# Scores of two attention kinds in the second token tile, computed in 64-row tiles of TensorE, both kinds at once

## The chip, the cores and the metric

The kernel runs on one core of a Trainium2 chip. The metric is device time in microseconds (us) of one launch, the median of three runs. A core has TensorE (PE in the profile, its weight loads PEld), VectorE (DVE), ScalarE (ACT), GpSimd (POOL) and SyncE (SP), each with an instruction queue of its own, tied to the others by semaphores alone.

## The reference

The launch computes two transformer blocks on 256 tokens in float32. Only the attention of the second block, run in each of its two layers, matters here. Its `nsa_mixer` has eight query heads over two key groups and three branches, compressed, selected and sliding:

```python
s = jnp.einsum('bqgrd,bgqmd->bgrqm', qi, kg).astype(jnp.float32) * scale   # selected
s = s - slopes[None, :, :, None, None] * dist_s
p_s = masked_softmax(s, mask_s)
o_s = jnp.einsum('bgrqm,bgqmd->bqgrd', p_s.astype(vg.dtype), vg)
s = jnp.einsum('bqgrd,bkgd->bgrqk', qi, kw).astype(jnp.float32) * scale    # sliding
...
o_w = jnp.einsum('bgrqk,bkgd->bqgrd', p_w.astype(vw.dtype), vw)
return gi[..., 0:1] * o_c + gi[..., 1:2] * o_s + gi[..., 2:3] * o_w
```

With 256 tokens both the selected and the sliding branch see every earlier key, so both are plain causal attention with a slope per head and 64 elements to a head (`NSA_DH = 64`). `mla_mixer` beside it is a third kind, with 96 elements to a head.

## The kernel before, in words

Every engine's program is written out by hand in one order. The 256 tokens are two tiles of 128 rows. The attention of a layer is a list of 26 units, `UNITS_2` (line 237), and each engine walks the list in a loop of its own, `attend`:

- K, the compressed branch, one unit for each tile;
- then for tile 0 the units S0 W0 S1 W1 S2 W2 S3 W3 M0 M1 M2 M3, then the same twelve for tile 1. S is the selected kind, W the sliding kind, M the latent kind; each unit has two heads. The position in the list, j, is 10 to 13 for M0 to M3 of tile 0, 14 to 21 for S0 to W3 of tile 1, and 22 to 25 for its M0 to M3. u is j plus an even offset.

A unit of tile 0 has 128 keys, one of tile 1 has 256. Its steps are: scores on TensorE into PSUM (line 1190, one matmul for each head; TensorE makes two passes of each float32 matmul, so the trace has two records for one matmul), logits on VectorE (2357, one instruction for each head adds the bias and takes the maximum; 2360 negates the maximum and announces `logits_ready`), exps on ScalarE (1692), turn on TensorE (1206, 128x128 transposes), copy out of PSUM on ScalarE (1702), value on TensorE (1232), output on VectorE (2403 reciprocal, 2413 gate, 2419 for S and W or 2421 for M).

The loops are staggered. TensorE does, for each j: scores(j), turn(j-2), value(j-3). VectorE does: logits(j), output(j-3). ScalarE does: copy(j-2), exps(j). The scores have two places in PSUM, 1024 columns each, used in turn (`(u % 2) * 1024`), so scores(j) waits for `logits_ready` of unit j-2: the place that it overwrites has been read.

Queries and keys of S and W lie on half of the partitions. `QTN` holds two heads in one tile, even head on partitions 0 to 63, odd head on 64 to 127; `KTN` holds for each head of a pair the keys on its own half and zeros on the other half. Before the change a matmul takes all 128 rows, zeros included. The two heads of a unit write to two halves of one PSUM bank (pitch 256 columns). M's heads take 96 of the 128 rows.

Elsewhere in the program (line 1337, the index scores of the first block) there are matmuls on 64 rows already: two heads on the two halves of the partitions, into two PSUM banks, 256 columns each, eight such pairs in the launch. They stand among full-height matmuls (1275) and transposes (1116).

Of the kernel before, what the change touches and what calls it, by code (L numbers as in the profile page):

```python
# [25 lines left out]
P = 128  # L26
# [6 lines left out]
HD = 64  # L33
# [51 lines left out]
G_LAYER = 26  # L85
# [131 lines left out]
def at(value, per, l):  # L217

    return value if l is None else value + per * l
# [5 lines left out]
def unit(kind, n, tile):  # L225

    keys = T if kind == "X" else 2 * NC if kind == "K" else P * (tile + 1)
    subs = 3 if kind == "A" else 4 if kind == "K" else 2

    return dict(kind=kind, n=n, tile=tile, keys=keys, subs=subs, pitch=512 if kind == "C" else keys, nk=1 if kind == "K" else keys // P,  # L230
                wide=kind == "A", mid=kind in "BKX")


# [6 lines left out]
U1, U2 = len(UNITS_1), len(UNITS_2) + len(UNITS_X)  # L240
# [7 lines left out]
def mids_before(u):  # L248
    return sum(x["mid"] for x in ALL_UNITS[:u])


def two_blocks_kernel(nc, a, out):
    ctx = ExitStack()
    with ctx:
# [3 lines left out]
        def sem(name):  # L258
            return ctx.enter_context(nc.semaphore(name))
# [14 lines left out]
        PS, PT, PO = ALL[:, 0:2048], ALL[:, 2048:3072], ALL[:, 3072:4096]  # L274
# [18 lines left out]
        def lbuf(x, u):  # L293

            if x["kind"] in "ABC":
                return w((W_L, W_L + 768, W_GB)[u % 3], 768)
            return w(W_L + 512 * (u % 3), 512)
# [24 lines left out]
        def ka(h):  # L322
            return QTA[:, 6 + h // 2, :] if h % 2 == 0 else P1[:, h // 6, T * (h // 2 % 3):T * (h // 2 % 3) + T]

        def qb(c):
            return P1[:, 0, 768 + c * T:768 + (c + 1) * T] if c < 3 else P1[:, 1, 768:1024]

        def kb(m):
            if m < 4:
                return P1[:, m % 2, C_BQ + T * (m // 2):C_BQ + T * (m // 2) + T]  # L330
            if m % 2 == 0:
                return P1[:, 1, 1024 + T * (m // 2 - 2):1024 + T * (m // 2 - 2) + T]
            return P1[:, m // 2 - 2, C_BQ + 512:C_BQ + 512 + T]

        def qc(n):
            return P1[:, n, C_CQ:C_CQ + T]
# [7 lines left out]
        def kc(s):  # L344
            return P1[:, s, C_BQ + 768:C_BQ + 1024]
# [47 lines left out]
        group_free = sem("group_free")  # L393
# [27 lines left out]
        scores_ready = sem("scores_ready")  # L421
        logits_ready = sem("logits_ready")
# [379 lines left out]
        def _(pe):  # L802
            mm = nc.tensor.matmul
# [295 lines left out]
            def branch_product(n, j, i, h, k, acts):  # L1099

                arrived(n)
                for c in range(k):
                    o = c * D + h * 512
                    last = mm(branch_bank(j, i, h), acts[:, c, i * P:(i + 1) * P], ring[:, n % RING, o:o + 512],  # L1104
                              start=(c == 0), stop=(c == k - 1))
                return last
# [36 lines left out]
            def query(x, s, i):  # L1143
                k, n = x["kind"], x["n"]
                q = slice(i * P, (i + 1) * P)
                if k == "A":
                    h = 4 * s + n
                    return [(QTA[:, h // 2, q], ka(h))]
                if k == "B":
                    h = 4 * s + n  # L1150
                    return [(qb(h // 2)[:, q], kb(h))]
                if k == "C":
                    return [(qc(n)[:, q], kc(s))]
                if k == "K":
                    return [(QTN[:, s, q], KBD[:, 30 * (s // 2):30 * (s // 2) + 30])]
                if k in "SW":
                    h = 2 * n + s
                    return [(QTN[:, h // 2, q], KTN[:, (4 if k == "S" else 8) + 2 * (h // 4) + h % 2, :])]
                if k == "M":
                    return [(QTM[:, 2 * n + s, q], KTM[:, 2 * n + s, :])]  # L1160
                return [(XQT[:, 4 * n + 2 * s + c, q], XK[n][:, 2 * s + c, :]) for c in range(2)]
# [17 lines left out]

            def attend(units, u0, l=None, between={}, behind_turn={}):  # L1180

                def scores(j):
                    x, u = units[j], u0 + j
                    if j >= 2:
                        pe.wait_ge(logits_ready, at(u - 1, U2, l))
                    for s in range(x["subs"]):
                        o = (u % 2) * 1024 + s * x["pitch"]
                        pairs = query(x, s, x["tile"])
                        for c, (q, k) in enumerate(pairs):
                            last = mm(PS[:, o:o + x["keys"]], q, k[:, 0:x["keys"]], start=(c == 0), stop=(c == len(pairs) - 1))  # L1190
                    last.then_inc(scores_ready, 1)

                def turn(j):
                    x, u = units[j], u0 + j
                    if x["mid"]:
                        pe.wait_ge(mixed_ready, at(mids_before(u) + 1, MIDS_2, l))
                    else:
                        pe.wait_ge(probs_ready, at(u + 1, U2, l))
                    single = x["wide"] or (j and units[j - 1]["wide"])
                    if j >= (1 if single else 2):  # L1200
                        pe.wait_ge(probs_out, at(u if single else u - 1, U2, l))
                    o = 0 if x["wide"] else (u % 2) * 512
                    for s in range({"B": 1, "K": 2}.get(x["kind"], x["subs"])):
                        for kb in range(x["nk"]):
                            c = s * P if x["kind"] == "K" else s * x["keys"] + kb * P
                            last = nc.tensor.transpose(PT[:, o:o + P], lbuf(x, u)[:, c:c + P], ident)  # L1206
                            o += P
                    last.then_inc(probs_turned, 1)

                def value(j):  # L1210
                    x, u = units[j], u0 + j
                    pe.wait_ge(probs_out, at(u + 1, U2, l))
                    if j >= 2:
                        pe.wait_ge(unit_done, at(u - 1, U2, l))
                    o = (u % 2) * 512
                    k = x["kind"]
                    if k == "X":
                        for c in range(4):
                            for kb in range(2):
                                n = 2 * (c // 2) + kb  # L1220
                                last = mm(PO[:, o + c * P:o + (c + 1) * P], XV[x["n"]][kb][:, c * P:(c + 1) * P],  # L1221
                                          PTS[:, u % 2, n * P:(n + 1) * P], start=(kb == 0), stop=(kb == 1))
                        last.then_inc(values_ready, 1)
                        return
                    dv = P if k == "B" else T if k == "K" else HD
                    blocks = [(s, kb) for s in range({"B": 1, "K": 2}.get(k, x["subs"])) for kb in range(x["nk"])]
                    for n, (s, kb) in enumerate(blocks):
                        pt = PTS[:, u % 2, n * P:(n + 1) * P]
                        first = n == 0 if k == "A" else kb == 0
                        final = n == len(blocks) - 1 if k == "A" else kb == x["nk"] - 1  # L1230
                        c = o if k == "A" else o + s * dv
                        last = mm(PO[:, c:c + dv], pt, values(x, s, kb), start=first, stop=final)  # L1232
                    last.then_inc(values_ready, 1)

                n = len(units)
                for j in range(n + 3):
                    if j in between:
                        between[j]()
                    if j < n:
                        scores(j)  # L1240
                    if 0 <= j - 2 < n:
                        turn(j - 2)
                    if j in behind_turn:
                        behind_turn[j]()
                    if 0 <= j - 3:
                        value(j - 3)
# [156 lines left out]
            for i in range(TT):  # L1403
                last = branch_product(P_BRA + 1, "c", i, 0, 2, XT[:, 6:8, :])
            last.then_inc(branch_done, 1)
            pe.wait_ge(branch_used, 1)
            for i in range(TT):
                last = branch_product(P_BRA + 1, "c", i, 1, 2, XT[:, 6:8, :])
            last.then_inc(panel_done, 1)
            pe.wait_ge(branch_used, 2)  # L1410
            for h in range(2):
                last = branch_product(P_BRA + 2, "b", 0, h, 4, XT[:, 2:6, :])
            last.then_inc(branch_done, 1)
            for h in range(2):
                last = branch_product(P_BRA + 2, "b", 1, h, 4, XT[:, 2:6, :])
# [18 lines left out]
            for l in range(LAYERS):  # L1434
# [91 lines left out]
                for g in range(2):  # L1526
                    last = mm(PO[:, 512 + g * HD:512 + (g + 1) * HD], HPAD[:, g, :], w2v, start=True, stop=True)
# [1365 lines left out]
```

## Time and profile before

| | us |
|---|---|
| median of three runs | 1697.09 |
| lowest, highest | 1696.93, 1698.31 |
| the profiled execution, its own time | 1696.81 |
| its span, first to last instruction | 1694.9 |
| TensorE busy (share of the span) | 1665.5 (98%) |
| VectorE busy | 1223.2 (72%) |
| ScalarE busy | 352.5 (21%) |
| mean granted TensorE clock | 0.998 |

The attention of the second block's first layer takes from about 831 us to 892 us of the span, that of the second layer from about 1313 to 1373 us. The profile has a record for each instruction, by engine and line. In the timeline a row's second number runs from the first start to the last end of the group, and matmul records overlap, since a matmul is started before the one ahead of it has drained: the spacing of starts tells what a matmul costs in a row of them. The chain of work that ended last counts each piece from the end of the piece before it, and so gives such costs directly.

### The profile page before, as it was taken

What the parts mean: (1) busy time and instruction counts of PE and PEld (TensorE: products, weight loads), DVE (VectorE), ACT (ScalarE), POOL (GpSimd) and SP (SyncE); (2) the same over time, 40 slices, a digit from 0 to 9 for tenths busy, and PEclk for the clock granted to TensorE, in tenths of its full rate; (3) what the DMA queues carried; (4) which work ended last, traced back from release to release, by engine and by line L of the source; (5) the groups of instructions that cost most, each with busy time, mean ns of one, the idle gap of its engine ahead of it and who ended that gap; (6) DMA issues with size and microseconds to landing.
All of it is one profiled execution on the core that took longest, in us unless ns stands there. A gap on an engine that the chain in (4) does not pass through costs nothing.

```text
span 1694.9 us, 22817 instructions
## 1 busy us (share of the span) xinstructions
PE 1665.5 (98%) x8726; PEld 1281.4 (76%) x8726; DVE 1223.2 (72%) x2230; ACT 352.5 (21%) x893; POOL 212.7 (13%) x139
## 2 busy tenths in 40 slices
PE   7999999999999999999999999999999999999998
PEld 6887488877847886477784969994687767699953
DVE  6777467976787777573376778996844685789995
ACT  2111000034511111112270212220012531222210
POOL 1222211121021212211001000002120000000021
PEclk9999999999999999999999999999999999999999
DMA  9685454524176555346513536444447206265440
GB/s 320 194 230 177 146 199 162 175 80 149 51 232 213 160 164 184 124 145 178 207 51 131 155 125 194 156 170 153 158 121 252 100 1 224 71 226 177 150 173 25
DMA packets 163755, 267.07 MB, mean 158 GB/s; under 512 B 4279, under 2 KB 106477, under 8 KB 163519
## 3 DMA queue, kind: packets, MB, share of 16 engines
q1 hardware_dynamic: 157902, 248.66, 43.8%
q0 software_dynamic: 5008, 15.91, 3.3%
q8 instruction: 70, 1.15, 0.3%
q10 hardware_dynamic: 736, 1.05, 0.3%
q14 instruction: 39, 0.31, 0.1%
HBM read 262.52 MB, written 2.03 MB: 156 GB/s over the span
## 4 chain that ended last, share of the span: by engine, by line
PE 90%; DVE 5%; DVEq 2%; issue 1%; ACT 1%; DMA 1%; SPq 0%; ACTq 0%
PE psum L1017 19%; PE psum L886 16%; PE psum L1065 13%; PE psum L952 12%; PE psum L844 7%; PE psum L1275 4%; PE psum L1481 3%; PE psum L1538 3%; PE psum L1190 3%; PE psum L1116 3%; PE psum L1232 2%; PE psum L825 2%; PE psum L1104 2%; PE psum L1206 1%; PE psum L1221 1%
## 5 line engine op out<-in xcount | busy, mean ns | idle before, releaser
L695 POOL TENSOR_TENSOR work<-ring,work 128x1024 f32<-128x1024 f32 (+2 forms) x59 | 147.4, 2499 | 791.5 <-DVE work L2199 791.5
L2191 DVE TENSOR_TENSOR work<-ring 128x1024 f32<-128x1024 f32 (+2 forms) x102 | 122.0, 1196 | 83.3 <-PE psum L1065 74.3
L1065 PE MATMUL psum<-ring,work 128*128 128x512 f32 x352 | 160.8, 592 | 0.0
L2195 DVE TENSOR_TENSOR ring<-ring 128x1024 f32<-128x1024 f32 (+2 forms) x104 | 131.7, 1267 | 7.7
L2199 DVE TENSOR_TENSOR work<-ring 128x1024 f32<-128x1024 f32 (+2 forms) x102 | 122.6, 1202 | 7.6
L1065 PEld LDWEIGHTS psum<-ring,work 128*128 128x128 f32 x352 | 66.4, 190 | 81.1 <-issue 79.9
L1065 PE MATMUL psum<-work 128*128 128x512 f32 x264 | 122.5, 592 | 0.0
L1017 PE MATMUL psum<-x_t,work 128*128 128x128 f32 x832 | 101.4, 275 | 0.0
L1017 PE MATMUL psum<-work,ring 128*128 128x128 f32 x832 | 101.4, 275 | 0.0
L1017 PE MATMUL psum<-x_t,ring 128*128 128x128 f32 x832 | 97.4, 275 | 1.6 <-ACT x_t L1610 1.6
L1017 PEld LDWEIGHTS psum<-x_t,work 128*128 128x128 f32 x832 | 97.1, 192 | 0.0
L1017 PEld LDWEIGHTS psum<-work,ring 128*128 128x128 f32 x832 | 97.1, 192 | 0.0
L1017 PEld LDWEIGHTS psum<-x_t,ring 128*128 128x128 f32 x832 | 95.0, 192 | 2.4 <-issue 2.4
L1065 PEld LDWEIGHTS psum<-work 128*128 128x128 f32 x264 | 49.7, 190 | 62.0 <-issue 60.3
L2823 DVE SCALAR_TENSOR_TENSOR work<-work 128x254 f32<-128x254 f32 (+1 forms) x176 | 83.5, 526 | 3.3
L886 PE MATMUL psum<-ring,work 128*128 128x256 f32 x352 | 83.2, 379 | 0.0
L886 PE MATMUL psum<-ring,x_t 128*128 128x256 f32 x352 | 81.7, 386 | 1.5 <-DMA ring<-in_ffn_w_gate_dram 1.3
L886 PE MATMUL psum<-work,x_t 128*128 128x256 f32 x352 | 82.9, 379 | 0.0
L1190 PE MATMUL psum<-work 128*128 128x256 f32 (+2 forms) x384 | 79.5, 338 | 0.3 <-DVE stat L2360 0.3
L886 PEld LDWEIGHTS psum<-ring,x_t 128*128 128x128 f32 x352 | 67.9, 194 | 12.2 <-DMA ring<-in_ffn_w_gate_dram 2.4
L1692 ACT ACTIVATE work<-work,stat 128x256 f32<-128x256 f32 (+1 forms) x136 | 61.6, 453 | 66.5 <-DVE stat L2360 65.6
L886 PEld LDWEIGHTS psum<-ring,work 128*128 128x128 f32 x352 | 66.9, 190 | 9.1
(304 smaller groups left out, 2865.6 us busy)
## 6 DMA issues: line engine op xcount, KB each, us to landing
ring<-in_ffn_w_up_dram SPq DMA_DIRECT2D x66, 1024.0 KB, 7.9
ring<-in_w_in_dram SPq DMA_DIRECT2D x21, 2048.0 KB, 7.9
ring<-in_ffn_w_down_dram SPq DMA_DIRECT2D x20, 2048.0 KB, 7.8
ring<-in_ffn_w_gate_dram SPq DMA_DIRECT2D x22, 1024.0 KB, 5.7
ring<-in_xa_wkv_dram SPq DMA_DIRECT2D x8, 2048.0 KB, 9.5
ring<-in_w_out_dram SPq DMA_DIRECT2D x6, 2048.0 KB, 10.9
ring<-in_xa_wq_dram SPq DMA_DIRECT2D x4, 2048.0 KB, 7.9
ring<-in_xa_wo_dram SPq DMA_DIRECT2D x4, 2048.0 KB, 11.3
```

Of the source, the lines that this page charges most:

```text
L695: nc.gpsimd.tensor_tensor(t4, quarters(n, chunks, pitch)[2], t2, ALU.subtract).then_inc(fourth_ready, 1)
L844: last = mm(share_bank(p), acts[p][:, q, :], rhs[:, i, :], start=(q == 0), stop=(q == KD // 2 - 1))
L886: last = mm(corners(j)[p], acts[p][:, i, :], rhs[:, i, :], start=(i == 0), stop=(i == KD // 2 - 1))
L952: last = mm(row_corners(j)[p][:, 0:pitch // 2], acts[p][:, i, :], rhs[:, i, :], start=(i == 0), stop=(i == KD // 2 - 1))
L1017: last = mm(corners(j)[p][:, c * P:(c + 1) * P], weights[:, i, c * P:(c + 1) * P], acts[p][:, i, :], start=(i == 0), stop=(i == KD // 2 - 1))
L1065: last = mm(sums[p], acts[p][:, q, :], rhs[:, i, :], start=(q == 0), stop=(q == KF // 2 - 1))
L1190: last = mm(PS[:, o:o + x["keys"]], q, k[:, 0:x["keys"]], start=(c == 0), stop=(c == len(pairs) - 1))
L1275: last = mm(row_corners(q + 1)[p], acts_of_gates[p][:, i, :], rhs[:, i, :], start=(i == 0), stop=(i == KD // 2 - 1))
L2191: v.tensor_tensor(t3, b22, b12, ALU.subtract)
L2195: v.tensor_tensor(b12, b12, b11, ALU.subtract)
L2199: v.tensor_tensor(t2, b22, b12, ALU.subtract).then_inc(forms_ready, 1)
L2823: last = v.scalar_tensor_tensor(dst, UP[:, q, 0:T - t], CWT[:, 2 - t, k:k + 1], dst, ALU.mult, ALU.add)
```

## The change

`unit` gives S and W units of tile 1 a pitch of 512 columns, so that the two heads of a unit write to two PSUM banks (0 and 1 for S, 2 and 3 for W). On TensorE, at the place of an S unit of tile 1, a new function issues the scores of that S unit and of the W unit behind it: four matmuls, each on 64 rows (the head's own half of the partitions, without the zeros). The W unit's own place issues no scores. The four matmuls wait for `logits_ready` of unit j-1 and for `group_free` (an earlier copy out of banks 1 and 3, made at the ninth unit ahead of them). Each unit still announces `scores_ready` behind its second matmul. Nothing changes on the other engines but the columns that the logits read.

```diff
-    return dict(..., pitch=512 if kind == "C" else keys, ...)
+    return dict(..., pitch=512 if kind == "C" or kind in "SW" and tile else keys, ...)
...
+                def scores_by_rows(j):
+                    u = u0 + j
+                    pe.wait_ge(group_free, at(H_WV + 2, G_LAYER, l))
+                    pe.wait_ge(logits_ready, at(u, U2, l))
+                    for t in (j, j + 1):
+                        x = units[t]
+                        for s in range(2):
+                            r = slice(HD * s, HD * s + HD)
+                            o = ((u0 + t) % 2) * 1024 + s * x["pitch"]
+                            (q, k), = query(x, s, 1)
+                            last = mm(PS[:, o:o + x["keys"]], q[r], k[r, 0:x["keys"]], start=True, stop=True)
+                        last.then_inc(scores_ready, 1)
+
                 def scores(j):
                     x, u = units[j], u0 + j
+                    if x["kind"] in "SW" and x["tile"]:
+                        if x["kind"] == "S":
+                            scores_by_rows(j)
+                        return
                     if j >= 2:
                         pe.wait_ge(logits_ready, at(u - 1, U2, l))
```

(`at(u, U2, l)` is the count of `logits_ready` when unit j-1 has announced; `at(u - 1, ...)` is that of unit j-2.)

TensorE's queue in the first layer, from the scores of S1 to those of S2 in tile 1, before:

```order
918 L1190 MATMUL psum<-work 128x256 [waits logits_ready]
919 L1190 MATMUL psum<-work 128x256
920 L1206 MATMUL psum<-ident_fours,work 128x128 [waits probs_out,probs_ready]
921 L1206 MATMUL psum<-ident_fours,work 128x128 x3
922 L1232 MATMUL psum<-work 128x64 [waits unit_done,probs_out]
923 L1232 MATMUL psum<-work 128x64 x3
924 L1190 MATMUL psum<-work 128x256 [waits logits_ready]
925 L1190 MATMUL psum<-work 128x256
926 L1206 MATMUL psum<-ident_fours,work 128x128 [waits probs_out,probs_ready]
927 L1206 MATMUL psum<-ident_fours,work 128x128 x3
928 L1232 MATMUL psum<-work 128x64 [waits unit_done,probs_out]
929 L1232 MATMUL psum<-work 128x64 x3
```

Every unit has its scores, then turn(j-2), then value(j-3). The same stretch after the change (lines are shifted: 1192 the new scores, 1223 turn, 1249 value):

```order
914 L1192 MATMUL psum<-work 128x256 [waits logits_ready,group_free]
915 L1192 MATMUL psum<-work 128x256 x3
916 L1223 MATMUL psum<-ident_fours,work 128x128 [waits probs_out,probs_ready]
917 L1223 MATMUL psum<-ident_fours,work 128x128 x3
918 L1249 MATMUL psum<-work 128x64 [waits unit_done,probs_out]
919 L1249 MATMUL psum<-work 128x64 x3
920 L1223 MATMUL psum<-ident_fours,work 128x128 [waits probs_out,probs_ready]
921 L1223 MATMUL psum<-ident_fours,work 128x128 x3
922 L1249 MATMUL psum<-work 128x64 [waits unit_done,probs_out]
923 L1249 MATMUL psum<-work 128x64 x3
```

The four score matmuls of a pair of units now stand together at its head, and the second unit's two have moved ahead of a turn and a value. (The shapes are those of the outputs; the rows that a matmul takes are not in this view.)

## Rows read from the trace of the kernel before

**Rows 1.** The page: span, busy time of TensorE and VectorE, the chain by engine.
```profile
span 1694.9 us, 22817 instructions
...
PE 1665.5 (98%) x8726; PEld 1281.4 (76%) x8726; DVE 1223.2 (72%) x2230; ACT 352.5 (21%) x893; POOL 212.7 (13%) x139
...
PE 90%; DVE 5%; DVEq 2%; issue 1%; ACT 1%; DMA 1%; SPq 0%; ACTq 0%
```

**Rows 2.** The chain in tile 1, first layer: start, us, what, records.
```profile
864.87 0.22 PE psum L1206 x2
865.08 0.39 PE psum L1232 x4
...
875.46 0.92 PE psum L1190 x4
876.38 0.44 PE psum L1206 x4
876.82 0.84 PE psum L1232 x8
877.66 0.92 PE psum L1190 x4
```

**Rows 3.** TensorE's timeline: start, us, engine line op, tiles, shape, records, [idle before].
```profile
863.78 1.08 PE L1190 MATMUL psum<-work 128*128 128x256 f32 x4
...
875.30 1.08 PE L1190 MATMUL psum<-work 128*128 128x256 f32 x4
876.22 0.60 PE L1206 MATMUL psum<-ident_fours,work 128*128 128x128 f32 x4
...
879.69 1.08 PE L1190 MATMUL psum<-work 128*128 128x256 f32 x4
```

**Rows 4.** The same in the second layer: scores of S0 and M0, tile 1.
```profile
1344.86 1.08 PE L1190 MATMUL psum<-work 128*128 128x256 f32 x4
...
1360.76 1.08 PE L1190 MATMUL psum<-work 128*128 128x256 f32 x4
```

**Rows 5.** VectorE's timeline: last logits of tile 0, then of tile 1.
```profile
864.93 0.17 DVE L2360 TENSOR_SCALAR stat<-stat 128x2 f32<-128x2 f32 x1
...
870.00 0.16 DVE L2403 RECIPROCAL stat<-stat 128x2 f32<-128x2 f32 x1
...
870.63 0.42 DVE L2357 CUSTOM_DVE_ANT_0 work<-psum,work 128x256 f32<-128x256 f32 x1
...
871.55 0.16 DVE L2403 RECIPROCAL stat<-stat 128x2 f32<-128x2 f32 x1
...
872.42 0.41 DVE L2357 CUSTOM_DVE_ANT_0 work<-psum,work 128x256 f32<-128x256 f32 x1
...
875.50 0.17 DVE L2403 RECIPROCAL stat<-stat 128x2 f32<-128x2 f32 x1 [0.25 <-PE psum L1232]
...
876.42 0.42 DVE L2357 CUSTOM_DVE_ANT_0 work<-psum,work 128x256 f32<-128x256 f32 x1
...
877.28 0.17 DVE L2360 TENSOR_SCALAR stat<-stat 128x2 f32<-128x2 f32 x1
```

**Rows 6.** The chain around an existing pair of 64-row matmuls (1337).
```profile
369.69 0.63 PE psum L1337 x4
370.33 0.59 PE psum L1116 x4
370.91 1.73 PE psum L1275 x8
372.64 0.44 PE psum L1116 x4
```

**Rows 7.** TensorE's timeline inside another such pair: first two records, last two.
```profile
353.38 0.49 PE L1337 MATMUL psum<-work 64*128 64x256 f32 x2
...
353.70 0.38 PE L1337 MATMUL psum<-work 64*128 64x256 f32 x2
```

**Rows 8.** Scores of the first block that did wait for VectorE's line 2360.
```profile
441.90 0.15 DVE L2360 TENSOR_SCALAR stat<-stat 128x1 f32<-128x1 f32 x1
...
442.11 0.48 PE L1190 MATMUL psum<-work 128*128 128x256 f32 x1 [0.28 <-DVE stat L2360]
```

More of the change, by code:

```diff
@@ L228, in unit @@
     subs = 3 if kind == "A" else 4 if kind == "K" else 2
-    return dict(kind=kind, n=n, tile=tile, keys=keys, subs=subs, pitch=512 if kind == "C" else keys, nk=1 if kind == "K" else keys // P,
+    return dict(kind=kind, n=n, tile=tile, keys=keys, subs=subs, pitch=512 if kind == "C" or kind in "SW" and tile else keys, nk=1 if kind == "K" else keys // P,
                 wide=kind == "A", mid=kind in "BKX")
```

## The prediction

> **What bounds the kernel now.** I read the page first: TensorE is busy for 98% of the span and carries 90% of the chain that ended last [rows 1]. So a change in TensorE's work counts only where TensorE itself is what ends last, and that is asked stretch by stretch. The chain inside tile 1 of the attention comes next. It is TensorE's own work without a gap: scores 0.92 us, turn 0.44, value 0.84, scores again, 2.20 us for one unit [rows 2]. The eight S and W units of tile 1 lie between the scores of S0 at 863.78 and those of M0 at 879.69, 15.91 us [rows 3], and take the same 15.90 in the second layer [rows 4]. Then I looked at how far VectorE is from being the bound there. Its logits take 0.92 us (from 870.63 to the reciprocal at 871.55) and the output of an S or W unit 0.87 (871.55 to 872.42), of an M unit 0.63 (870.00 to 870.63) [rows 5]. That is 1.79 us of 2.20, and it waits 0.25 us for value's result before each output [rows 5]. VectorE has slack, but only 0.4 us in a unit, and it stands in a loop with TensorE.
>
> **Part 1, the 64-row matmuls.** A pair of units has 2 x 0.92 = 1.84 us of score matmuls now [rows 2]. The pairs at line 1337 show what 64 rows do. Two matmuls are four records, two passes each. The first two records start together at 353.38, the last two together at 353.70 [rows 7]: the two halves of the array do work at once. (The first records are 0.10 longer for the weight load ahead of them; less that, the steps are one pass's time.) In the chain such a pair takes 0.63 us and makes the four transposes behind it 0.15 slower (0.59 against 0.44) [rows 6]. A full-height pass of 256 columns is 1.73 / 8 = 0.216 us [rows 6]. So of 0.63 + 0.15 = 0.78 us, 0.43 are the two double passes, 0.20 lie ahead of them and 0.15 behind: the array empties before tiles of another height start and again on the way back. Four matmuls in one go cost four double passes, 0.86, plus these 0.35 once: 1.21 us against 1.84. Were TensorE alone the bound, a pair would gain 0.63 us, eight pairs in two layers 5.0 us.
>
> **Part 2, the new wait.** Scores of S and W now start together, so both places in PSUM must have been read: the wait is for the logits of unit j-1 instead of j-2. Today these are not ready when TensorE gets there. TensorE reaches the scores of S0 at 863.78 [rows 3], while the logits of the unit ahead (M3 of tile 0) end at 864.93 + 0.17 = 865.10 [rows 5]. Behind the waiting matmul in TensorE's queue stand turn(j-2) and value(j-3), and VectorE's output(j-3), which stands ahead of the logits of the W unit, waits for that very value. So a loop closes: scores of a pair, turn, value, output(j-3) on VectorE, logits of W, scores of the next pair. I follow it with these durations. From the end of line 2360 to the first full pass 0.15 us: 442.05 to 442.11, with a record 0.10 longer than the plain 0.38, which is the weight load [rows 8, 7]; the emptying of the array is over by then, since TensorE stands idle. The two units' scores: done 0.43 and 0.86 after that, and 0.15 to get back to full height, 1.01 in all. Turn and value: 0.22 and 0.39 for units of tile 0, 0.44 and 0.84 for units of tile 1 [rows 2]. From the end of a TensorE group to VectorE's first instruction on it 0.20 (875.30 to 875.50, and 876.22 to 876.42) [rows 3, 5]. Logits 1.03 until line 2360 has ended (876.42 to 877.45) [rows 5].
>
> First pair (S0, W0): starts at 865.10 + 0.15 = 865.25, that is 1.47 late. Full height at 866.26, turn(M2) and value(M1) until 866.87, seen by VectorE at 867.07, output(M1) until 867.70, logits(W0) until 868.73. (Logits of S0 are ready to start at 865.88 and are over by 866.80, so they don't hold it up.)
>
> Second pair (S1, W1): starts at 868.88. Full height 869.89, turn(S0) and value(M3) until 870.72, output(M3) until 871.55, logits(W1) until 872.58.
>
> Third pair: starts at 872.73. Full height 873.74, turn and value at full length until 875.02, output(W0) 875.22 to 876.09, logits(W2) until 877.12.
>
> Fourth pair: starts at 877.27. Full height 878.28, then two rounds of turn and value, 1.28 each, and the scores of M0 at 880.84; their wait is the old one, on unit j-2 (S3, logits over at about 878.9), and costs nothing. Before, they started at 879.69. So a layer **loses 1.15 us**: TensorE's groups get 4 x (1.84 - 1.01) = 3.3 us shorter, and it stands waiting at the four heads for about 1.5 + 1.4 + 0.7 + 1.0 = 4.6 us (the 0.1 between is a small delay of today's that goes). From M0 on the order is the old one and TensorE-bound, so nothing is given back or added later.
>
> **Part 3, the rest.** The pitch of 512 changes where logits read, not how much: no cost, and the rows of line 1337 are of matmuls into two banks as well. The wait for `group_free` was satisfied many units earlier, and while TensorE waits for the logits anyway its extra instruction is hidden; where it weren't, it would cost some 0.05 to 0.1 us a pair. No DMA moves. The second layer has the same spacing [rows 4], so the sum is taken twice: 2 x 1.15 = +2.3 us. Against the profiled execution's own 1696.81 us this is 1699.1; that execution lies 0.28 below the median, and on the median of 1697.09 it gives **1699.4 us**, +0.14%.
>
> The bounds: returning to full height could cost 0.20 as entering does, and starting after the wait 0.21 if the emptying isn't hidden; both on the loop, 0.11 x 4 x 2 = +0.9 us. With nothing behind the four matmuls and 0.10 ahead of them (0.2 less together) it would be -0.2 x 8 = -1.6 us. VectorE's output at 0.92, as it stands in the unit at 875.50 [rows 5], adds 0.05 in one pair of a layer, +0.1. The forecast's own range is 1697.8 to 1700.4.
>
> **Rivals.**
>
> *The scores gain and the wait doesn't bind* (faster). If VectorE announced its logits earlier than TensorE comes back, the 0.63 us a pair of part 1 would be had: -5.0 us, 1692.1. Against it is the 865.10 of the logits beside TensorE's 863.78, a row of the very wait, and the order on VectorE, which puts output(j-3) ahead of the W logits. The Trainium skill (TensorEngine Tiling (Array Packing), Theoretical Speedup) gives up to twofold for a small dimension of at most 64. By that rule alone the pair's 1.84 us would halve and the kernel would come to 1697.1 - 8 x 0.92 = 1689.7. The trace shows little of it in a short go: 0.78 us with both borders [rows 6] against four full-height passes, 0.86.
>
> *The four matmuls don't overlap as two do* (slower). Line 1337 never has more than one matmul for each half. Here W's matmuls follow on the same halves. Each waiting for the one ahead of it, all eight passes alone, a pair's block would be 0.86 us longer, on the loop: +2.3 + 8 x 0.86 = +9.2, 1706.3. It decides from some 0.14 us a pair on, above which the time leaves what counts as no change. Rows 7 speak against it: the second passes already follow the first ones on the same half, and in step. Between lies a case in which passes keep strict order in the queue, so that a matmul's second pass holds back the first pass of the next one: five slots in place of four, +0.22 x 8 = +1.7, 1701.1. The Trainium skill (TensorE: Matmul & The Clock Gate, Part 3, The mechanism) says that matmuls start and end strictly in program order. If the two passes of a matmul count as two such, rows 7 disagree: two slots for a pair and not three.
>
> *The change doesn't do what it says.* If the loop is cut elsewhere (VectorE has its outputs done ahead of TensorE's block in some pairs), the waits shrink to about half, 2.3 us a layer: -1.2 us a layer, 1694.8. I see no such cut in the order.
>
> **How the numbers follow.** What a measurement here can tell from no change is about 0.2%, 3.4 us. The forecast (loss of about 2.3 us) gets 0.74. The gain in full 0.04, half of it 0.04. No overlap 0.08, strict order 0.06, and 0.04 for a loop longer than worked out (a copy or exps on ScalarE in it). Faster by over 0.2% is the full gain and a little of the half: 0.05. Slower by over 0.2% (above 1700.5) takes the no-overlap case, most of strict order, the longer loop and the forecast's edge: 0.20. Within 0.2%: 0.75. The range of 1697.0 to 1702.5 leaves out both gains and the no-overlap case, 0.16, and a little of the longer loop.
>
> **What would show it.** Right: the first of the new score groups in tile 1 starts about 1.5 us later against the units ahead of it, the four starts are 3.6, 3.85 and 4.5 us apart, each with TensorE idle ahead of it and VectorE's line 2360 (2377 after) as releaser; from the fourth to M0's scores 3.6 us; eight records in four steps of 0.216 us; M0 to the end of the attention as before. Wrong: no idle time ahead of the new groups (the wait doesn't bind), or steps of the passes above 0.216 (no overlap), or idle time between scores and turn in tile 1, which would put ScalarE into the loop.

## The result, and the profile after

The changed kernel takes 1702.07 us (median of six runs, 1701.65 to 1706.21) against 1697.05 us (six runs), a ratio of 1.0034 with a 95% interval of 1.0021 to 1.0047: slower by 5.0 us, more than twice the 2.3 us of the forecast, and above the 3.4 us up to which the prediction speaks of no change. In a later comparison (the run "changed again" below, eleven runs, 27 of the kernel before) it took 1700.55 us against 1696.84, 1.0023 with 1.0014 to 1.0031, +3.7 us. The kernel before spread over 1.5 us there, the changed one over 2.8.

The page of the changed kernel's first profiled execution (1706.21 us, the slowest of its six):

```profile
span 1704.4 us, 22825 instructions
...
PE 1669.3 (98%) x8726; PEld 1282.6 (75%) x8726; DVE 1223.4 (72%) x2230; ACT 351.4 (21%) x893; POOL 212.4 (12%) x139
```

Beside [rows 1] the counts of TensorE's matmuls and of VectorE's instructions are the same, and so are their shares; a difference of half a percent can't be read from there. In all, the trace has eight instructions more (22825 against 22817), one for each pair of units. What they are is told below, where the idle time is filled. TensorE's timeline of the second layer's tile 1 shows the new order (1192 new scores, 1223 turn, 1249 value, 1207 the other scores; start, us, group, [idle before]):

```profile
1349.43 1.48 PE L1192 MATMUL psum<-work 64*128 64x256 f32 x8 [1.30 <-DVE stat L2377]
...
1354.11 2.08 PE L1192 MATMUL psum<-work 64*128 64x256 f32 x8 [0.66 <-DVE stat L2377]
...
1360.35 2.08 PE L1192 MATMUL psum<-work 64*128 64x256 f32 x8
1362.36 1.11 PE L1223 MATMUL psum<-ident_fours,work 128*128 128x128 f32 x4
...
1366.57 1.14 PE L1192 MATMUL psum<-work 64*128 64x256 f32 x8 [0.78 <-DVE stat L2377]
1367.63 0.66 PE L1223 MATMUL psum<-ident_fours,work 128*128 128x128 f32 x4
...
1370.25 1.08 PE L1207 MATMUL psum<-work 128*128 128x256 f32 x4
```

Two things stand here. TensorE waits ahead of the pairs for VectorE's line 2377, the end of the logits, as the prediction said. And the same eight records take 2.08 us in the second and third pair and 1.14 in the fourth, the same four transposes 1.11 and 0.66. The busy time by stretches tells why (length, then busy time and records of PE, PEld, DVE, ACT and POOL, then the granted clock as a share of 2.4 GHz, then the DMA):

```profile
865.40:868.80 3.40, 3.40 (x16) 2.71 (x17) 1.39 (x8) 1.48 (x8) 0.00 (x0) 0.50 0.00 0
868.80:883.00 14.20, 11.86 (x99) 10.46 (x98) 10.52 (x58) 10.21 (x34) 0.00 (x0) 1.00 0.01 2
1340.00:1350.00 10.00, 8.13 (x61) 6.80 (x62) 8.46 (x58) 7.49 (x33) 0.00 (x0) 1.00 0.08 29
1350.10:1363.70 13.60, 12.94 (x60) 10.42 (x57) 7.18 (x38) 6.24 (x23) 0.00 (x0) 0.50 0.00 1
1363.70:1378.00 14.30, 13.52 (x106) 12.47 (x106) 10.48 (x59) 10.90 (x35) 0.00 (x0) 1.00 0.01 2
```

TensorE ran at 1.2 GHz for 3.4 us in the first layer and for 13.6 us in the second, each time starting inside the first pair's block, right behind the longest wait. The kernel before keeps 2.4 GHz through both attentions. The prediction has no term for that.

### The profile page after: what moved, and what is told of

Its sections match the earlier page's. It is cut to its first block, busy times and chain, and to the rows that moved or that the text cites. A ratio compares the mean times of both kernels' runs of the same rounds, so it can differ in the third digit from the quotient of the medians.

```text
span 1704.4 us, 22825 instructions
## 1 busy us (share of the span) xinstructions
PE 1669.3 (98%) x8726; PEld 1282.6 (75%) x8726; DVE 1223.4 (72%) x2230; ACT 351.4 (21%) x893; POOL 212.4 (12%) x139
## 3 DMA queue, kind: packets, MB, share of 16 engines
q8 instruction: 70, 1.15, 0.3%
## 4 chain that ended last, share of the span: by engine, by line
PE 90%; DVE 6%; DVEq 2%; issue 1%; ACT 1%; DMA 0%; SPq 0%; ACTq 0%
PE psum L1017 19%; PE psum L886 16%; PE psum L1065 13%; PE psum L952 11%; PE psum L844 7%; PE psum L1292 3%; PE psum L1498 3%; PE psum L1555 3%; PE psum L1116 3%; PE psum L1249 2%; PE psum L1207 2%; PE psum L825 2%; PE psum L1104 2%; PE psum L1223 1%; PE psum L1238 1%
## 5 line engine op out<-in xcount | busy, mean ns | idle before, releaser
L1620 ACT ACTIVATE work<-psum 128x512 f32<-128x512 f32 (+4 forms) x66 | 34.7, 550 | 180.6 <-PE psum L1116 180.3
```

## Theories and experiments

Theory A: the loop of waits costs TensorE some 1.2 to 1.5 us a layer, and the idle time that it makes brings the clock down to 1.2 GHz behind it in some executions; this is the rest. Rival B: matmuls on 64 rows bring the clock down by themselves. Rival C or D: the 64-row matmuls cost time and the wait doesn't. Times below are medians, each with the ratio to the kernel before on the same chip.

### The changed kernel again

No edit.

> The changed kernel once more, for a second profiled execution and more times. Theory A: idle time ahead of every pair again, 0.45 to 1.3 us as in the first trace, M0 of tile 1 about 1.45 us late in a layer where the clock stays up, and stretches at 1.2 GHz that differ in place and length from the first trace's; the time follows them: 1700 without any, 1701.7 with about 3.4 us of them, up to 1706 with more.

1700.55 us (1699.66 to 1702.46). This execution (1701.12 us) has a first layer without a drop. First M3 of tile 0 of the kernel before, to measure from, then TensorE's timeline here:

```profile
862.27 0.66 PE L1190 MATMUL psum<-work 128*128 128x128 f32 x4
```

```profile
862.27 0.66 PE L1207 MATMUL psum<-work 128*128 128x128 f32 x4
...
865.24 1.13 PE L1192 MATMUL psum<-work 64*128 64x256 f32 x8 [1.29 <-DVE stat L2377]
866.31 0.44 PE L1223 MATMUL psum<-ident_fours,work 128*128 128x128 f32 x2
...
868.97 1.13 PE L1192 MATMUL psum<-work 64*128 64x256 f32 x8 [1.10 <-DVE stat L2377]
...
872.92 1.13 PE L1192 MATMUL psum<-work 64*128 64x256 f32 x8 [0.45 <-DVE stat L2377]
...
877.54 1.13 PE L1192 MATMUL psum<-work 64*128 64x256 f32 x8 [0.78 <-DVE stat L2377]
...
881.22 0.87 PE L1207 MATMUL psum<-work 128*128 128x256 f32 x3
```

Both start M3's scores at 862.27, and M0's of tile 1 stand at 881.22 against 879.69 [rows 3]: this layer loses 1.53 us with the clock up all the way. The second layer had 3.4 us at half clock:

```profile
1348.10:1351.50 3.40, 3.40 (x18) 2.72 (x16) 1.50 (x9) 1.67 (x8) 0.00 (x0) 0.51 0.02 5
1351.50:1366.00 14.50, 12.35 (x100) 10.88 (x100) 10.54 (x58) 9.89 (x33) 0.00 (x0) 1.00 0.01 2
```

Two clean layers come to 2 x 1.53 = 3.1 us, 1699.9; five of the eleven runs lie there, at 1699.66 to 1699.99, and the others up to 2.6 us above. The expectation of clean runs at 1700 and of runs with drops above them holds. (Only the profiled executions show their clock; for the others the drops are read off their times.) The first six runs, 1701.65 and more, all lie above that level.

### The 64-row matmuls alone

Each unit issues its own two 64-row matmuls at the old place, with the old wait.

```diff
-                    pe.wait_ge(group_free, at(H_WV + 2, G_LAYER, l))
-                    pe.wait_ge(logits_ready, at(u, U2, l))
-                    for t in (j, j + 1):
+                    if units[j]["kind"] == "S":
+                        pe.wait_ge(group_free, at(H_WV + 2, G_LAYER, l))
+                    pe.wait_ge(logits_ready, at(u - 1, U2, l))
+                    for t in (j,):
...
-                        if x["kind"] == "S":
-                            scores_by_rows(j)
+                        scores_by_rows(j)
                         return
```

> The 64-row matmuls and the wider pitch alone: every S and W unit of tile 1 issues its own two scores at its old place and waits for the logits of unit j-2, as before the change. Theory A (TensorE's new idle time at the pair heads costs the time, directly and because the granted clock falls to 1.2 GHz after it): TensorE never waits, the clock stays at 2.4 GHz through tile 1, and a block costs 0.78 to 0.83 us against 0.92, so a gain of 0.1 us for each of 16 units less what small waits on ScalarE take: 1695.5 to 1696.6. Rival B (matmuls on 64 rows by themselves bring the clock down): stretches at 1.2 GHz in tile 1 without idle time ahead of them, and 1698 or more.

1695.57 us (1695.20 to 1696.24), ratio 0.9993, interval 0.9984 to 1.0002: within the expectation, and by its interval not told apart from no change. In the trace the gain is plain: units are 2.06 us apart instead of 2.20 [rows 3], and the clock does not fall in either layer. Not every unit gains: the first turn of full length in tile 1 stands waiting for ScalarE's exps (line 1709; the first row below), and from M3's scores to those of M0 a layer is 0.66 us shorter, not 8 x 0.14.

```profile
867.70 0.66 PE L1223 MATMUL psum<-ident_fours,work 128*128 128x128 f32 x4 [0.22 <-ACT work L1709]
...
872.81 0.70 PE L1193 MATMUL psum<-work 64*128 64x256 f32 x4
873.45 0.65 PE L1223 MATMUL psum<-ident_fours,work 128*128 128x128 f32 x4
873.94 1.00 PE L1249 MATMUL psum<-work 128*128 128x64 f32 x8
874.87 0.70 PE L1193 MATMUL psum<-work 64*128 64x256 f32 x4
```

Rivals C and D fall: the matmuls bring a little time and cost none. B falls as well, as far as 64 rows alone are meant.

### The order and the wait alone

The changed kernel with full-height matmuls (all 128 rows, zeros included) in the pairs.

```diff
-                            r = slice(HD * s, HD * s + HD)
...
-                            last = mm(PS[:, o:o + x["keys"]], q[r], k[r, 0:x["keys"]], start=True, stop=True)
+                            last = mm(PS[:, o:o + x["keys"]], q, k[:, 0:x["keys"]], start=True, stop=True)
```

> The new order and wait alone: four full-height score matmuls (128 rows, zeros included) of S and W together, waiting for the logits of unit j-1. Theory A: a pair's block is 1.73 us instead of 1.01, all of it on the loop, so +7 to +8 us from the loop alone (1704 to 1705), with idle time of about 1 us ahead of each pair as in the changed kernel, and where the clock falls 1.7 us or more on top: 1704 to 1712. Rival B (64 rows bring the clock down): the same +7.5 us and no stretch at 1.2 GHz in tile 1, 1704 to 1705. Rival C (the wait costs nothing and only the 64-row matmuls are slow): 1697.

1707.76 us (four runs, 1706.93 to 1708.19), ratio 1.0063, interval 1.0049 to 1.0077. The waits are those of the changed kernel, and the clock fell in the first layer of this trace:

```profile
866.40:869.80 3.40, 3.40 (x12) 2.64 (x10) 1.06 (x6) 0.41 (x3) 0.00 (x0) 0.50 0.00 0
869.80:887.00 17.20, 14.84 (x106) 13.57 (x105) 10.92 (x59) 11.03 (x36) 0.00 (x0) 1.00 0.01 1
```

```profile
1353.07 1.96 PE L1191 MATMUL psum<-work 128*128 128x256 f32 x8 [1.30 <-DVE stat L2376]
...
1357.48 1.97 PE L1191 MATMUL psum<-work 128*128 128x256 f32 x8 [1.11 <-DVE stat L2376]
```

So 64 rows aren't needed for a drop: rival B is out. And the full block's extra time comes out at the end, as it must if it lies on a loop: the starts of the first two pairs are 4.41 us apart against 3.73.

### The loop cut on VectorE

In tile 1 VectorE takes the logits of S and W one behind the other, then the two outputs. Maxima, sums and reciprocals get eight places instead of four (`f` below is 0 or 4), or the exps of W would write over sums still to be read.

```diff
+def stat_column(x, u):
+    return 4 * (u // 4 % 2) if x["kind"] in "SWM" else 0
...
-                    if j < n:
+                    ahead = FIRST_TOGETHER <= j < 22 and units[0]["kind"] == "K"
+                    if ahead and j % 2 == 0:
+                        logits(j)
+                        logits(j + 1)
+                    elif j < n and not ahead:
                         logits(j)
```

With `FIRST_TOGETHER = 14`, S0 of tile 1:

> The changed kernel with the loop cut on VectorE: in tile 1 the logits of S and W both stand ahead of the outputs of j-3 and j-2 (logits, logits, output, output), with maxima and sums in eight places instead of four so that this is safe. TensorE is as in the changed kernel. Theory A: the first pair of a layer still waits about 1.3 us, the second about 0.3, the third and fourth not at all, and their period is 3.8 us against 4.39: -2.2 us from the loop, 1694.9 if the clock stays up, some 1.7 us more in executions where it falls behind the first pair. Rival B (64 rows): the clock still falls in the third and fourth pair. Rival D (the cost is in the 64-row matmuls, not in the wait): no better than the changed kernel, 1701 to 1702.

1698.05 us, ratio 1.0006, interval 0.9997 to 1.0015, and widely spread, 1695.43 to 1699.97. The loop did what was expected:

```profile
865.58 1.13 PE L1197 MATMUL psum<-work 64*128 64x256 f32 x8 [1.30 <-DVE stat L2383]
...
868.49 1.14 PE L1197 MATMUL psum<-work 64*128 64x256 f32 x8 [0.28 <-DVE stat L2383]
...
872.01 1.13 PE L1197 MATMUL psum<-work 64*128 64x256 f32 x8
...
875.79 1.14 PE L1197 MATMUL psum<-work 64*128 64x256 f32 x8
...
879.47 0.87 PE L1212 MATMUL psum<-work 128*128 128x256 f32 x3
```

The period of the late pairs is 3.78 us (3.8 expected). The lowest run, 1695.43, is 0.5 us above the expected 1694.9 of a clean one; this trace has 3.4 us at half clock behind the first pair of the second layer, and most runs lie 1.5 to 4.5 us above the lowest. Only the wait ahead of the first pair is still long here, 1.30 us, which points at that one.

With `FIRST_TOGETHER = 12`, M2 of tile 0:

> The loop cut on VectorE as in the third experiment, but two units earlier (from M2 of tile 0 on), so that the logits that the first pair waits for are done some 0.6 to 0.9 us sooner. Theory A: idle of about 0.4 us ahead of the first pair and 0.8 ahead of the second instead of 1.3 and 0.3, none after; 0.3 us a layer less than with the later cut, and the clock falls less often or not at all: 1694.7 to 1695.5 where it stays up. Rival: what brings the clock down is the sum of the idle time and not the length of one piece, then the times are spread as in the third experiment, 1695 to 1699.

1695.13 us (1694.77 to 1695.63), ratio 0.9989, interval 0.9980 to 0.9997, and a spread of 0.9 us. The idle time is 0.52 and 0.78 us ahead of the first two pairs, and no drop is in the trace:

```profile
864.47 1.14 PE L1197 MATMUL psum<-work 64*128 64x256 f32 x8 [0.52 <-DVE stat L2383]
...
867.87 1.14 PE L1197 MATMUL psum<-work 64*128 64x256 f32 x8 [0.78 <-DVE stat L2383]
```

In sum that is 1.30 us against the 1.58 of the version before, which alone would be thin ground to give up the rival on the sum of idle time; the run with only the first wait filled, below, has 2.33 us of it in a layer and no drop either. So it is not the sum.

### Idle time filled

The changed kernel with its loop of waits, but ahead of the wait for unit j-1's logits TensorE transposes the identity into a bank that is free instead of standing still.

```diff
+                    pe.wait_ge(logits_ready, at(u - 1, U2, l))
+                    for _ in range({14: 10, 16: 8, 18: 3, 20: 5}[j]):
+                        nc.tensor.transpose(PS[:, 512:512 + P], ident, ident)
                     pe.wait_ge(logits_ready, at(u, U2, l))
```

> The changed kernel with TensorE's idle time filled: ahead of the wait for the logits of unit j-1 it makes 10, 8, 3 and 5 transposes of the identity into a bank that is free (extra work whose result nobody reads), 0.11 us each, a little less than the waits of 1.3, 1.1, 0.45 and 0.78 us at the four pairs. The loop of waits stays as it is. Theory A (the clock falls because TensorE stands idle): no stretch at 1.2 GHz in either attention, every time close to the lowest of the changed kernel, 1699.6 to 1700.3, with a spread of about 1 us instead of 3. Rival B (the clock falls for another reason, the order or the 64 rows): stretches as before, 1700 to 1703 with the same spread.

1699.25 us (1698.75 to 1700.41), ratio 1.0013, interval 1.0004 to 1.0022. No drop:

```profile
860.00:882.00 22.00, 21.30 (x171) 17.88 (x171) 17.16 (x103) 15.92 (x58) 0.00 (x0) 1.00 0.01 1
1342.00:1364.00 22.00, 21.22 (x171) 17.84 (x170) 16.86 (x98) 16.13 (x60) 0.00 (x0) 1.00 0.01 3
```

Extra work in the same order, and the clock stays up and the spread is smaller, 1.7 us against 2.8: it is the standing still that brings the clock down. The trace and the spread carry this reading, and the two runs that follow, which were measured side by side. The lower ratio does not carry it: the intervals of 1.0013 and 1.0023 overlap, and the edit changes one thing more. The time is 0.4 us below the expectation's lower end, and the trace shows where that comes from:

```profile
862.67 0.66 PE L1210 MATMUL psum<-work 128*128 128x128 f32 x4
...
869.20 1.13 PE L1195 MATMUL psum<-work 64*128 64x256 f32 x8
...
881.27 0.43 PE L1210 MATMUL psum<-work 128*128 128x256 f32 x1
```

From M3's scores to M0's it is 18.60 us, 1.18 more than before (862.27 to 879.69 [rows 3], 17.42) and not 1.53: each pair starts 0.09 us sooner behind the end of the logits. The chain of work shows it, in the changed kernel (first block) and in this one (second block). Each "issue" is the time from the end of the logits to the pair's first record, in which the engine waits for nothing that the profile shows:

```profile
865.11 0.14 issue
865.24 1.13 PE psum L1192 x8
```

```profile
865.51 0.04 issue
865.56 1.13 PE psum L1195 x8
```

The reason is not that TensorE was busy. Ahead of the third pair of the version with `FIRST_TOGETHER = 12` it stands idle for 0.02 us only, as it does ahead of the third pair here, and still that pair starts 0.15 us behind its logits, which end at 871.08 + 0.17 = 871.25:

```profile
871.08 0.17 DVE L2383 TENSOR_SCALAR stat<-stat 128x2 f32<-128x2 f32 x1
...
871.40 1.14 PE L1197 MATMUL psum<-work 64*128 64x256 f32 x8
```

What differs is the instruction that waits. In the changed kernel two waits stand ahead of the pair's first matmul, `group_free` and `logits_ready`, and the one on the logits (line 1185 of its kernel) has an instruction of its own in TensorE's queue; these are the eight that the kernel before does not have:

```profile
L1185 PEldq EVENT_SEMAPHORE  x8: 51/51/51, 865.1 to 1361.4; - x8
```

In the filled version `group_free` and the extra instruction's wait stand ahead of the transposes, and the pair waits for its logits without an instruction in between. The version of full-height matmuls has both waits again, and the same 0.14 us ahead of its first pair ("1352.93 0.14 issue" in its chain). No run takes `group_free` away by itself.

Then one wait at a time. Only the first pair's filled (`{14: 10, 16: 0, 18: 0, 20: 0}`):

> As the kernel with all idle time filled, but only the wait ahead of the first pair of a layer is filled (10 transposes); the waits of about 1.1, 0.45 and 0.78 us at the other three pairs stay empty. Theory A1 (it is the 1.3 us ahead of the first pair, behind tile 0 where TensorE already waits often, that brings the clock down): the clock stays at 2.4 GHz, 1699.3 to 1700.0 with a spread of about 1 us. Theory A2 (any idle time of about 1 us does it): stretches at 1.2 GHz behind the second pair, a spread of 2 us and more up to 1702.

1699.89 us, 1699.58 to 1700.40, ratio 1.0016, interval 1.0007 to 1.0025. Waits of 1.10, 0.45 and 0.78 us are left, 2.33 us in sum, and the clock stays up in both layers:

```profile
869.20 1.13 PE L1195 MATMUL psum<-work 64*128 64x256 f32 x8 [1.10 <-DVE stat L2380]
```

```profile
860.00:882.00 22.00, 19.25 (x153) 16.37 (x153) 17.06 (x101) 15.81 (x58) 0.00 (x0) 1.00 0.01 1
```

All but the first filled (`{14: 0, 16: 8, 18: 3, 20: 5}`):

> The counterpart: the first pair's wait of 1.3 us stays empty, those of the second to fourth pair are filled (8, 3 and 5 transposes). Theory A1: the clock falls behind the first pair in part of the executions, as in the changed kernel, but never for longer than one stretch of 3.4 us in a layer: 1699.4 to 1702. Theory A2: fewer drops than in the changed kernel.

1700.67 us, 1699.52 to 1702.40, ratio 1.0021, interval 1.0012 to 1.0030. The spread of the changed kernel is back, 2.9 us beside the 0.8 of the run before, on the same chip. In the first layer of the trace the clock falls inside the first pair's block behind the wait, which takes 1.85 us instead of 1.13:

```profile
865.54 1.85 PE L1195 MATMUL psum<-work 64*128 64x256 f32 x8 [1.30 <-DVE stat L2380]
```

```profile
860.00:882.00 22.00, 20.24 (x151) 16.85 (x151) 15.82 (x95) 15.13 (x56) 0.00 (x0) 0.92 0.01 1
```

So it is the 1.3 us ahead of the first pair. It comes right behind tile 0, where TensorE already waits a little in each unit, as a stretch of the kernel before shows:

```profile
851.00:863.78 12.78, 11.97 (x90) 10.21 (x90) 10.86 (x73) 9.96 (x43) 0.00 (x0) 1.00 0.44 163
```

The 1.10 us of the second pair follow a pair's work without a gap. That this difference is what makes the first wait the harmful one was not tried.

### A version that beats both

Where VectorE is still behind from tile 0, the pairs are not used: S0 to W1 issue their 64-row matmuls unit by unit with the old wait, the last two pairs go together, and VectorE has its logits ahead from S1 on.

```diff
+                    alone = j < FIRST_PAIR
-                    pe.wait_ge(logits_ready, at(u, U2, l))
-                    for t in (j, j + 1):
+                    pe.wait_ge(logits_ready, at(u - 1 if alone else u, U2, l))
+                    for t in (j,) if alone else (j, j + 1):
...
-                        if x["kind"] == "S":
+                        if x["kind"] == "S" or j < FIRST_PAIR:
                             scores_by_rows(j)
```

With `FIRST_TOGETHER, FIRST_PAIR = 16, 18`:

> A version that should beat both: the first two pairs of tile 1, where VectorE is still behind from tile 0, issue their 64-row scores unit by unit with the old wait, the last two go as pairs, and from S1 on VectorE takes both logits ahead of both outputs. Theory A: no new idle time on TensorE, clock at 2.4 GHz, a layer gains 0.13 us for each of four units and 0.5 us for each of two pairs less 0.1 to 0.4 of small waits: 1.1 to 1.3 us a layer, 1694.2 to 1694.7. If the loop is not what costs, it is at the level of the rows-alone kernel, 1695.6, or above.

1694.79 us (1694.07 to 1695.76), ratio 0.9987, interval 0.9978 to 0.9996: faster than the kernel before by 2.3 us and than the changed one by 6 us or more (by the ratios). It is 0.1 us above the expectation's upper end. One small wait is left in the first layer, 0.30 us:

```profile
871.67 1.13 PE L1198 MATMUL psum<-work 64*128 64x256 f32 x8 [0.30 <-DVE stat L2384]
```

With `FIRST_TOGETHER = 12` in it:

> The mixed version (first two pairs of tile 1 unit by unit with 64-row matmuls and the old wait, last two as pairs) with VectorE taking both logits ahead of both outputs already from M2 of tile 0 on. Theory A: the small wait of 0.3 us that is left ahead of the third pair goes, 0.1 to 0.3 us a layer: 1694.3 to 1694.8, as good as the mixed version or a little better, clock at 2.4 GHz.

1694.95 us (1694.64 to 1695.40), ratio 0.9988, interval 0.9979 to 0.9996: the same within the noise, 0.15 us above what was expected. The small wait is 0.22 us now and has not gone:

```profile
871.39 1.14 PE L1198 MATMUL psum<-work 64*128 64x256 f32 x8 [0.22 <-DVE stat L2384]
```

## Why the prediction was wrong, step by step

**What bounds the kernel.** Right: TensorE is the bound in tile 1, and what is put on its path comes out at the end.

**Part 1, the 64-row matmuls.** Right in mechanism. The second pair's matmuls follow on the same halves without a gap: eight records take 1.13 us in the clean layer against 0.70 of four, 0.43 more, four double passes and not five. Strict order and the missing overlap are both out. The alone-version gains 0.14 us in a unit of full length where the rows gave 0.92 - 0.78 = 0.14. In it the turn starts 0.64 us behind the first of the four records (872.81 to 873.45), of which the two double passes are 0.43. The Trainium skill (TensorEngine Tiling (Array Packing), Key Properties) says that a change of the tiling mode drains TensorE; the trace agrees with its 0.2 us on top of the passes.

**Part 2, the new wait.** Right in place, order and sign. The four waits were given as 1.5, 1.4, 0.7 and 1.0 us up to the first full pass; the records show idle times of 1.29, 1.10, 0.45 and 0.78, each short of that by 0.2 to 0.3: they begin only when the last record ahead has ended, and the first record behind has its weight load in front. From the first record to the turn it is 1.07 us in every pair at full clock. The starts were to be 3.6, 3.85 and 4.5 us apart and are 3.73, 3.95 and 4.62, each 0.1 us more.

**The steps that failed.** Two things were put at nothing, and both cost.

The first is in part 3, in the words "while TensorE waits for the logits anyway its extra instruction is hidden; where it weren't, it would cost some 0.05 to 0.1 us a pair". The extra instruction is the one that waits for the logits, so it is not hidden. Line 2360 and the matmul behind it in [rows 8], from which the start behind the wait was taken (0.06 us to the first record), have no such instruction between them. In the new pairs the start takes 0.14 to 0.15 us, 0.09 more for each of eight pairs. Over four pairs this makes the 1.15 us of a layer 1.15 + 4 x 0.09 = 1.51, and 1.53 is measured. With the wait filled, where the instruction lies elsewhere, 1.18 came out, and 1699.25 us in all against the forecast's 1699.4. That part of the loss, 8 x 0.09 = 0.7 us or a little more, is closed.

The second is in part 2: "I follow it with these durations". All of them, the block, turn and value behind each wait, were taken from rows at 2.4 GHz. The text counted the idle time as time lost, 4.6 us a layer, and didn't ask what TensorE's clock does behind it. A drop in one layer costs 1.3 us (1347.86 to 1352.90 between the first two pairs in the run "changed again", 5.04 us against 3.73), in the first trace 1.5 us in the first layer and 4.8 in the second, where M3's scores start at 1346.45 and M0's at 1370.25, 6.37 us more than the 17.42 of before, of which 1.53 are the loop. The sum closes: 1.53 + 1.53 + 1.5 + 4.8 = 9.4 us, and the two profiled executions are 1706.21 - 1696.81 = 9.4 apart.

In the median the 5.0 us of the first comparison are then, as an estimate, 2.3 as forecast, 0.7 for the extra instruction and, as what is left, 2.0 of clock; the 3.7 of the second are 2.3, 0.7 and 0.7.

**The rivals.** None held. The gain of 5 us would need the loop cut: with it the late pairs run at 3.78 us, nearly the 3.77 of TensorE alone (1.21 and twice 1.28). The rival in which VectorE's order cuts the loop by itself was wrong too: the waits are there at all four pairs. What was missing was a rival on the clock, and the profile before held no row against it: in both attentions it shows 2.4 GHz and no wait on TensorE longer than 0.3 us ahead of tile 1. The chance of 0.20 for a time above 1700.5 us rested on other mechanisms.

## What to carry to other kernels

A wait that is moved one unit forward has to be followed round the loop of both engines before the saved work is counted; here it was 4.6 us of waiting for 3.3 us saved in a layer by the prediction's sum, and turning two steps on the other engine took it all back (1695.13 us). Where two waits stand ahead of one matmul, look which of them gets the extra instruction: if it is the one that ends last, the instruction lies on the path. Where a change makes TensorE stand idle behind a stretch in which it already waits often, count the price of the lower clock too, look at the spread of the times for it, and test it by filling the wait with work nobody needs. Two short goes of small tiles pay the emptying of the array twice; put them together only where the other engine is ahead.

## What was not expected of the hardware

An idle time of 1.3 us was enough to have TensorE at 1.2 GHz for 3.4 us, starting inside the block behind it, and once for 13.6 us. It did not do so each time: of the four layers in the changed kernel's two traces three have a drop, and by their times 12 of its 17 executions have at least one. An idle time of 1.10 us ahead of the second pair did not do it by the times of eleven runs and one trace, 0.52 and 0.78 us neither. The Trainium skill (TensorE: Matmul & The Clock Gate, HAM oscillation — how this bites in real kernels) describes a clock that falls back after idle time between matmuls. The trace agrees with the fall; the waits of the page's worked example are longer than the 1.3 us here, and for the length the trace decides.

Why the version with `FIRST_TOGETHER = 14` seems to have fallen in ten of its eleven runs and the changed kernel, with the same first wait, in six of the eleven of the same comparison, was not settled. Nor was the reason for the 13.6 us. One reading is that the moment of the wait within the launch counts, since the versions reach it at slightly different times; no run here tells.
